# First gate/up job of each feed-forward with eight plain products, a third raw weight buffer, and x prepared in two parts

## What is computed

```python
def _rmsnorm(x, g):
    y = xf * lax.rsqrt(jnp.mean(xf * xf, axis=-1, keepdims=True) + EPS)
    return (y * g.astype(jnp.float32)).astype(x.dtype)

def _swiglu(x, w_gu, w_down):
    a, b = jnp.split(x @ w_gu, 2, axis=-1)
    return (jax.nn.silu(a) * b) @ w_down

for i in range(DEPTH):
    x = x + 0.5 * _swiglu(_rmsnorm(x, norm_g[i, 0]), ffn_gu[i, 0], ffn_down[i, 0])
    ...
    x = x + m
    x = x + 0.5 * _swiglu(_rmsnorm(x, norm_g[i, 2]), ffn_gu[i, 1], ffn_down[i, 1])
```

## Time and profile before

| | us |
|---|---|
| median of 3 runs | 2686.99 (2685.89 to 2690.67) |
| profiled execution, own time | 2693.75 |
| span of the profile | 2692.2 |
| mean granted TensorE clock | 0.963 |
| busy: PE, DVE, ACT, POOL | 2511.5, 1832.6, 1109.4, 824.0 |
| feed-forwards 0, 1, 2, 3 | about 12 to 430, 940 to 1360, 1360 to 1753, 2258 to 2660 |

### The profile page before, as it was taken

How to read it: one execution, slowest core, us unless ns; L and a number is a source line. 1 busy time by engine, 2 the same in 40 slices (tenths; PEclk the granted TensorE clock), 3 DMA queues, 4 the chain that set the end, 5 groups by cost and what they waited for, 6 DMA issues and landing times.

```text
span 2692.2 us, 48445 instructions
## 1 busy us (share of the span) xinstructions
PE 2511.5 (93%) x19519; PEld 2409.5 (89%) x19519; DVE 1832.6 (68%) x2560; ACT 1109.4 (41%) x1802; POOL 824.0 (31%) x659
## 2 busy tenths in 40 slices
PE   4889999999999978899988999999999997889998
PEld 4889999898989878899978999989998997889997
DVE  7766776645464687767786777677557657867774
ACT  4434443424242453444453444444433344434443
POOL 3433332202020243333342343312530452423431
PEclk7999999999999989999989999999999999999999
DMA  3233334525242322233222333331122120223331
GB/s 93 74 89 109 91 99 138 184 79 184 81 182 90 138 63 79 87 103 98 91 68 81 96 99 102 103 97 50 48 70 79 35 69 15 79 80 98 99 97 69
DMA packets 295369, 247.95 MB, mean 92 GB/s; under 512 B 9429, under 2 KB 275853, under 8 KB 295153
## 3 DMA queue, kind: packets, MB, share of 16 engines
q1 hardware_dynamic: 280800, 197.32, 24.4%
q0 software_dynamic: 14352, 47.58, 5.1%
HBM read 218.81 MB, written 26.05 MB: 91 GB/s over the span
## 4 chain that ended last, share of the span: by engine, by line
PE 78%; DVE 13%; ACT 4%; issue 3%; DMA 1%; POOL 1%; ACTq 0%; SPq 0%; POOLq 0%; DVEq 0%
PE ps L1547 29%; PE ps L1173 18%; PE ps L1568 13%; PE ps L1357 4%; DVE wl L2136 4%; PE ps L980 3%; ACT wh L1695 2%; DVE parts L2123 2%; DVE x L2221 2%; PE ps L1068 1%; PE ps L1091 1%; PE ps L1077 1%; DVE xcl L2131 1%; PE ps L1301 1%; PE ps L1367 1%
## 5 line engine op out<-in xcount | busy, mean ns | idle before, releaser
L1547 PE MATMUL ps<-xch,wh 128*128 128x260 f32 x2464 | 724.7, 294 | 123.9 <-DVE x L2221 53.3
L1547 PE MATMUL ps<-xch,wl 128*128 128x260 f32 x2464 | 716.7, 291 | 0.0
L1547 PE MATMUL ps<-xcl,wh 128*128 128x260 f32 x2464 | 716.3, 291 | 0.0
L1547 PEld LDWEIGHTS ps<-xch,wh 128*128 128x128 f32 x2464 | 485.2, 197 | 139.2 <-DVE x L2221 59.5
L2136 DVE TENSOR_TENSOR wl<-raw,wh 128x512 fp32r<-128x512 f32 (+1 forms) x440 | 475.6, 1089 | 152.2 <-ACT wh L1695 149.5
L1547 PEld LDWEIGHTS ps<-xcl,wh 128*128 128x128 f32 x2464 | 484.9, 197 | 0.1
L1547 PEld LDWEIGHTS ps<-xch,wl 128*128 128x128 f32 x2464 | 484.4, 197 | 0.0
L1695 ACT ACTIVATE wh<-raw 128x512 fp32r<-128x512 f32 (+1 forms) x440 | 342.1, 796 | 214.1 <-PE ps L1547 124.5
L1568 PE MATMUL ps<-hh,wh 128*128 128x260 f32 x1408 | 284.2, 283 | 4.7 <-DVE x L2221 4.7
L1568 PE MATMUL ps<-hl,wh 128*128 128x260 f32 x1408 | 284.2, 283 | 0.0
L1568 PE MATMUL ps<-hh,wl 128*128 128x260 f32 x1408 | 283.8, 283 | 0.0
(11 more groups left out here) (387 smaller groups left out, 4175.0 us busy)
## 6 DMA issues: line engine op xcount, KB each, us to landing
raw<-in_ffn_gu_dram SPq DMA_DIRECT2D x176, 512.0 KB, 5.1
raw<-in_ffn_down_dram SPq DMA_DIRECT2D x96, 384.0 KB, 3.7
raw<-in_ret_w_in_dram SPq DMA_DIRECT2D x48, 512.0 KB, 4.4
s_ring<-in_state_ret_dram POOLq DMA_DIRECT2D x32, 512.0 KB, 6.7
out_dram<-s_ring POOLq DMA_DIRECT2D x32, 512.0 KB, 3.6
raw<-in_gdn_w_in_dram SPq DMA_DIRECT2D x32, 512.0 KB, 5.1
raw<-in_ffn_down_dram SPq DMA_DIRECT2D x32, 256.0 KB, 2.9
raw<-in_ret_w_out_dram SPq DMA_DIRECT2D x16, 512.0 KB, 4.1
```

The costliest lines, as they stand in the source:

```text
L1547: m_ = nc.tensor.matmul(o, w_, r_, start=m in (1, 2, 5) and t == 0 and n == 0, stop=t == KP - 1 and n == 2, skip_group_check=m in (3, 4, 6 ...
```

## The change

It has these parts.

- **Job 0 whole.** `is_whole(0)`: job 0 of each feed-forward is made of eight plain products: gate (weights A, result Y, banks 6 and 7) and up (weights L, banks 2 and 3), 8 K-tiles, 2 token halves, 3 passes: 96 matmuls in the new `whole`, in tile groups (0,1,2,3), (4,5), (6), (7). It needs no weight sums, no sums of x, and splits 2 x 1024 columns of weights in place of 7 x 512.
- **x in two parts.** The four plain columns of a pair of tiles are split first (`x_gained` on ACT, `x_low_of` on DVE, a new buffer pair `xbh`, `xbl` for one of them). Sums (`x_mixed`) and the other four columns (`x_split`) follow: in ffn(0) all behind the start of job 0, in the others only those of the last pair of tiles.
- **Root earlier.** The norm sum uses banks 0 and 1; product 1 of job 1 waits for its root. Job 0 is scaled in `whole_scaled` and multiplied in `whole_product` during job 1.
- **Third raw buffer.** Loads go to slot j % 3 (the third lies in `parts_r`) and wait for job j - 3; job 2's waits for the first late split of x.
- **Group L later.** On DVE group L of a gate/up job behind a down job is split after XA and XB.
- Block 7 takes the place of block 2 in every other down job; the h ring is rotated in ffn(2); transposes of the input use other banks. Job 0's L uses blocks 4 and 6; block 4 is also the last one that job 37 reads.

The names and the loads:

```diff
+WHOLE_BLOCKS = {"A": (2, 3), "L": (4, 6)}
...
-    return "A124L" if j == 0 else "A12L4"
+    return "AL" if is_whole(j) else "AL214" if is_whole(j - 1) else "A12L4"
...
-    return (3, 5, 4) if is_gate(j - 1) or not down_blocks(j - 1)[0] else (0, 1, 2)
+    return (3, 5, 4) if is_gate(j - 1) or not down_blocks(j - 1)[0] else (0, 1, 7)
...
+        raw_third = parts_r[:].rearrange("p c t -> p (c t)")[:, 0:SLOT]
...
-                    s = j % 2
+                    s = j % 3
...
-                    elif j >= 2:
-                        sp.wait_ge(blk_low, blocks_split(f, j - 2))
+                    elif j == 2 and f != 2:
+                        sp.wait_ge(xc_low, KP * f + 1)
+                    elif j >= 3:
+                        sp.wait_ge(blk_low, blocks_split(f, j - 3))
```

On PE:

```diff
+                def whole(part, n):
+                    to_, m = {"A": (Y, n % 2), "L": (UP, n % 2)}[part]
+                    at_ = WHOLE_BLOCKS[part][m] * BLOCK + n // 2 * P
+                    hi_w, lo_w = all_h[:, at_:at_ + P], all_l[:, at_:at_ + P]
+                    pe.wait_ge(blk_low, blocks_split(f, 0, part))
+                    pe.wait_ge(xb_low, 3 * (KP * f + n // 2) + (3 if n % 2 else 2))
+                    for h in range(2):
...
+                            m_ = nc.tensor.matmul(to_[:, h, :], w_, r_, start=n == 0 and i == 0, stop=n == KT - 1 and i == 2)
...
+                if f == 2:
+                    v(f"XA.{NJ - 1}", f - 1)
+                for tiles_ in ((0, 1, 2, 3), (4, 5), (6,), (7,)):
+                    if tiles_ == (7,):
+                        norm_sum(NORM_IN[f])
+                    for part in "AL":
...
+                        for n in tiles_:
+                            whole(part, n)
```

On DVE, `before_ffn`:

```diff
+                if n:
+                    x_low_of(f, n - 1)
+                if n == 5:
+                    block_split(f, 0, "A")
+                if f and n and n % 2 == 0:
+                    x_mixed(f, n // 2 - 1)
+                if f and n % 2 and n > 1:
+                    x_split(f, n // 2 - 1)
                 if n == KT - 1:
...
+                    x_low_of(f, n)
                     block_split(f, 0, "L")
```

On DVE, `ffn`:

```diff
+                    if is_whole(j):
+                        low("A")
+                        begin = 0 if f == 0 else KP - 1
+                        for t in range(begin, KP):
+                            x_mixed(f, t)
+                            if t > begin:
+                                x_split(f, t - 1)
+                        x_split(f, KP - 1)
+                        low("L")
+                        dve.wait_ge(ssq_root, NORM_IN[f] + 1)
+                        nc.vector.reciprocal(rinv[:], rinv[:]).then_inc(ssq_inv, 1)
...
                     if is_gate(j):
-                        if j and not gate_before:
+                        if not gate_before:
+                            block_split(f, j, "L")
                             block_split(f, j, "4")
...
                         first(p)
                         h_low(p)
-                        low("2Lyz")
+                        low("2yz")
                         continue
                     low("Ax")
                     if ending:
                         tile_done(f, 2 * m)
-                    low("1y")
+                    low("1Ly")
```

More of the change, by code:

```diff
@@ L115, in is_gate, with is_whole @@
     return 0 <= j < NJ and JOBS[j][0] == "G"
+def is_whole(j):
+    return j == 0
 def groups_of(j):
@@ L143, in uses_of @@
         return {down_blocks(j)[i]: f"P{i}.{j}" for i in range(len(JOBS[j][2]))}
+    if is_whole(j):
+        return {b: f"{name}.{j}" for group, name in (("A", "Y"), ("L", "E")) for b in WHOLE_BLOCKS[group]}
     uses = {b: f"{m}.{j}" for m, b in PRODUCT_BLOCK.items()}
@@ L167, in ffn_t_names @@
     for j in range(NJ):
-        before = [f"4.{j - 1}"] if is_gate(j - 1) else []
-        if is_gate(j):
+        before = [f"4.{j - 1}"] if is_gate(j - 1) and not is_whole(j - 1) else []
+        if is_whole(j):
+            out += [f"Y.{j}", f"E.{j}"]
+        elif is_gate(j):
             first, *rest = (f"{m}.{j}" for m in gate_order(j))
@@ L202, in ffn_a_names @@
     for j in range(NJ):
-        before = is_gate(j - 1)
+        before, products = is_gate(j - 1), is_gate(j) and not is_whole(j)
         if before:
             out.append(f"silu.{j - 1}")
-        if is_gate(j):
+        if products:
             out.append(f"m1.{j}")
@@ L209, in ffn_a_names @@
             out.append(f"hh.{j - 1}")
-        if is_gate(j):
-            out += [f"m5.{j}", f"u2.{j}"] if j == 0 else [f"u2.{j}", f"m5.{j}"]
+        if products:
+            out += [f"u2.{j}", f"m5.{j}"]
     return " ".join(out)
@@ L775, in ffn @@
                     nxt2 = after(*nxt) if nxt else None
-                    if nxt and is_gate(nxt[1]):
+                    if nxt and is_gate(nxt[1]) and not is_whole(nxt[1]):
                         block_sum(*nxt, "2")
@@ L780, in ffn @@
                         square_added(NORM_OUT[f], 2 * (j - LATE - 1))
-                    if nxt2 and is_gate(nxt2[1]):
+                    if nxt2 and is_gate(nxt2[1]) and not is_whole(nxt2[1]):
                         block_sum(*nxt2, "1")
@@ L1574, in down @@
                                 turn_y(2 * (j - LATE - 1) + 1)
-                            if i == 0 and n == 0 and is_gate(j - 1):
+                            if i == 0 and n == 0 and is_gate(j - 1) and not is_whole(j - 1):
                                 product(j - 1, 4)
@@ L1610, in ffn @@
                         product(j, m)
-                        if m == 1 and is_gate(j - 1):
+                        if m == 1 and is_gate(j - 1) and not is_whole(j - 1):
                             product(j - 1, 4)
@@ L1753, in high @@
                                 block_split(*nxt, group)
+                    if is_whole(j):
+                        high("A")
+                        for t in range(0 if f == 0 else KP - 1, KP):
+                            x_split(f, t)
+                        high("L")
+                        root_of(NORM_IN[f])
+                        continue
                     if is_gate(j):
+                        if is_whole(p):
+                            block_split(f, j, "2")
+                            block_split(f, j, "1")
                         if gate_before:
@@ L1816, in tile_done @@
                 squared(NORM_OUT[f], t)
+                if f == 1 and t % 2 and t > 1:
+                    x_split(f + 1, t // 2 - 1)
                 if f == 3 and t % 2 == 0 and t:
@@ L2298, in tile_done @@
                     scaled_low(f // 2, t)
-                if f == 1 and t % 2 == 0:
-                    x_mixed(f + 1, m, 0)
-                    x_split(f + 1, m, False)
-                if f == 1 and t % 2:
-                    for i in range(1, 4):
-                        x_mixed(f + 1, m, i)
+                if f == 1:
+                    if t:
+                        x_low_of(f + 1, t - 1)
+                    if t and t % 2 == 0:
+                        x_mixed(f + 1, m - 1)
+                    if t % 2 and t > 1:
+                        x_split(f + 1, m - 1)
+                    if t == KT - 1:
+                        x_low_of(f + 1, t)
                 if f == 3:
```

308 lines of the change are left out of this document (147 added, 161 removed).

## The result

| | before | changed |
|---|---|---|
| median of the runs | 2687.44 us (2685.89 to 2690.67, 4 runs) | 2638.92 us (2635.11 to 2642.53, 4 runs) |
| the profiled execution | 2693.75 us | 2639.59 us |
| its granted clock | 0.963 | 0.974 |

The ratio is 0.9818, 95% interval 0.9801 to 0.9835: 48.5 us less between the medians, 54.2 between the profiled executions. The forecast was 2635 us.

What follows compares the result with a forecast made beforehand. PE was taken as the bound (busy 93% of the span), so only its idle time and lower-clock time could be won. Terms -23 - 12 - 17 = -52 us against the median 2686.99 gave 2635 us, range 2602 to 2670.

Steps and rivals of the forecast that it cites:

- the passages: 16 changes from a down to a gate/up job (jobs 6, 8, 10, 12 of four feed-forwards): -32 us, idle and clock.
- the starts: From the last down job or the mixer's last additions to job 5 of each feed-forward: -17 us forecast.
- the rest: Jobs 15 to 37 of the four feed-forwards: -3 us forecast.
- Term 1: PE's waits for additions to x shrink with group L split behind them: -23 us, between 0 and -42.
- 1.5 us of idle left before product 2 of job 8: Sign that the forecast is right; 0.3 us would show closed passages, 3.0 us the slower case.
- Term 2: Half the clock loss in four stretches of alternating down and gate/up jobs is won: -12 us, between 0 and -25.
- Term 3: Earlier product 6 of job 1 at the feed-forwards' starts: -17 us, between -35 and +6.
- Then come L (1.22), 72 of the 96 matmuls: ffn(3) and ffn(1): work counted after tile 7's plain columns, 19 us to product 6 of job 1; -5 and -4 us.
- PE starts 6 us after the end: ffn(2): L of job 0 waits for block 4, delaying PE after the last down job; net 0.
- Passages closed: Rival: 0.3 us idle left at the passages and the clock stays up; -82 us, 2605 us, chance 0.14.
- Starts give nothing: Rival: DVE's sums meet POOL at every step, starts end where they do now; -22 us, 2665 us, chance 0.19.
- Slower, sums holding DVE twice: Rival: both POOL sums precede the additions, PE 0.6 us later at each of 16 passages; 2702 us, chance 0.08.

Runs made afterwards that it cites:

- held loads: Changed kernel with each load of job j waiting for the splits of job j-2, not j-3: 2635.78 us, ratio 0.9797; also called late loads.
- held sums: Changed kernel with POOL's two early sums held at each down-to-gate/up passage until DVE has split group 4: 2618.57 us, ratio 0.9727.
- Order alone: Kernel before, with only DVE's split of group L moved behind the additions to x; profiled twice: 2635.87 us (ratio 0.9791) and 2636.6 us (0.9802).
- the copy ahead of the silu: Changed kernel with ACT's copy in job 1 ahead of job 0's silu and DVE's group 2 ahead of the reciprocal: 2621.51 us, one run.

## Why the prediction was right, and where not

**The time** was right (2635 for 2638.92), and that is in part luck: the passages gave 12 us more than forecast, the starts 6 and the rest 2 less, and the mixers took 2.5 more.

**Term 1, idle time at the passages.** The mechanism came out as written: additions directly behind group 2, the first POOL sum holding it, no wait for L at product 7. "1.5 us of idle left before product 2 of job 8" is 0.98. I had set the additions 0.85 us sooner against the start of `hh`, and they are 1.0 sooner; the rest is that PE runs out of work 0.36 us later than I had it. The term was -20 for the 16 passages; the waits there fell from 43.5 to 15.8 us, by 27.7. That the stretches lose only 19.9 us of idle time is no confirmation: 4.4 us of the old waits lay ahead of the cuts, and waits for `kept` in jobs 13 and 14 grew by 3.3. All idle time behind additions to x came to 22.4 us (15.8 and 6.6), where "about 30" had been set down. Of the 3 us forecast outside the passages, the waits of 1.40 and 2.09 us between the last down jobs of ffn(1) are gone, but the rest of the four feed-forwards is only 1.0 us shorter. That the third buffer was to blame for the part not won was half true: held loads won nothing (1600.5 us), because the sum then held group A; held sums won 9.8. Order alone gave 49.3 and 44.2 of 56.6 us.

**Term 2, the clock, mis-sized: -12 forecast, some -19.5 measured.** The step that failed was "neither as the 2.35 that stand there now nor absent ... I take half". The runs put it otherwise. With 0.98 to 1.01 us of idle at each passage the clock is 1.00 in every stretch of the seven profiles that have this pattern (one passage of the 112 excepted: there a load made POOL's first sum start 0.18 us behind group 2, which took 0.68 us, and PE did not wait); with 2.35 and, before job 12, 3.4 to 3.9 it is 0.93 to 0.95, with 3.2 it is 0.93 to 0.94. In between it is mixed, and not by the idle times alone: late loads (0.8 to 2.6 us) had 0.98, 0.98, 1.00, 1.00, order alone 1.00 four times in one profile and 0.96, 0.98, 1.00, 1.00 in the other, and held sums, with no wait for x at all, had 0.98 in one of four.

**Term 3, the starts: -17 forecast, -11.2 measured**, of which 5.4 come with the order of L alone, since the stage ends at job 5's additions. By the forecast's own measure, the start of product 6 of job 1, they are -9.4, -0.7, +1.9 and -1.2 us (from the start of the program, the mixer's last additions, and in ffn(2) the last down job's end on PE). ffn(0): product 6 at 52.93 for the forecast 54 (62.35 before), by the step named, the sums beside PE's job 0. ffn(1) and ffn(3): -4 and -5 forecast, -1.2 and -0.9 measured. The step that failed is "Then come L (1.22), 72 of the 96 matmuls": L was taken as following tile 7's plain columns, but it stands behind DVE's late columns, which wait for ACT, and two sums of POOL's stretch the splits. With L in front these two stages are 4.5 and 4.4 us shorter, more than was missing. One loss was not forecast at all: from product 6 of job 1 to PE's last matmul before product 2 of job 6 the same 372 matmuls take 1.4 to 2.0 us longer in each feed-forward (201.5 us in all before, 208.0 now, 202.6 with the order alone). Nearly all of it is idle time (12.0 and 17.8 us), behind copies to `kept`. Which part of the change causes it no run shows. ffn(2): "PE starts 6 us after the end", 6.64 measured, and 0 for the stage, +0.1 measured. The number was right, by luck, and its cause wrong: not block 4 but the sums of x ahead of the additions.

**Rivals.** Passages closed: it took one more wait. Starts give nothing: true for three of four. Slower, sums holding DVE twice: this happened as soon as L was put back in front (2701 us; the 2702 of that rival are added up from other terms); in the change L's place keeps the second sum off the path. The mechanism "a DVE group more than one POOL sum late" was thus real, and one line from the result.

**Not in the forecast:** the mixers, +2.5 us in this execution and -17.2 to +9.4 against the 1018.7 us of before in the other profiles. It is why differences below 1% were read from the stages.

## What to carry to other kernels

Put what PE waits for next ahead of what it needs later, on the in-order engine that does both: here that alone gave 44 to 49 of the 56.6 us of a long change. A buffer that lets an engine run ahead also moves its work in time, so look at what it then runs beside, and hold it (with a wait on the step behind) if it stands in the way of the critical engine. Cut the span at the same program steps in each kernel and compare the stages: the total mixes in the clock of stages that nobody touched.

## What was not expected of the hardware

The clock did not follow the idle share. Of 91 us, 5.7 us idle in pieces of 1 us cost nothing (1.00), while 10.5 to 13.0 us in pieces of 2.35 to 3.9 us went with a clock of 0.93 to 0.95. So where the 16 waits fell by 27.7 us, some 19.5 us of clock came back with them. What lies between 1 and 2.35 us is not settled: the first passages of the order alone, with the same waits within 0.3 us (0.8 to 1.0 and one of 3), had 1.00 in one profile and 0.96 in the other.

The lock between VectorE and GpSimd has a fine structure that decides here. A DVE split with two SBUF inputs that began 0.53 us into a POOL sum took 1.78 us instead of 0.68, and the sum 1.76 instead of 1.29; an addition to x, one of whose inputs is in PSUM, took its usual 1.29 us for two beside the second sum (121.42 to 122.71). The Trainium skill ("SBUF — State Buffer", section on the two separate sides) confines the lock to VectorE operations with two SBUF inputs, or in a mode with two ports; both rows agree.

The mixers' time, with the same instructions, ran from 498.1 to 516.9 us (retention) and from 503.3 to 513.7 (gated-delta). It is the clock: PE's idle time in them is 3.5 to 3.6 and 11.9 to 12.0 us in all 14 profiles, and the granted clock 1.00 in the shortest, 0.96 (retention) and 0.97 (gated-delta) in the longest. And it falls there without a wait: with the sums held, the stretch from 484 to 494 us was granted 0.52 with PE busy for all of its 10.00 us, where the profile of the copy ahead of the silu has 1.00 at the same steps (487 to 497 us). Why it falls in one execution and not in another no run here shows.
